# Gates projected with channels on the partitions, probabilities divided by their sums on GpSimd, masks in bias rows, a new beginning and a finer selection in a two-layer streaming encoder step

## What is computed

```python
h = rmsnorm(x, g_norm[l]);  p = split_proj(h @ w_in[l])
# A: every query keeps its top-k keys by an indexer's score, and attends to them
score = einsum('bqh,bqhl->bql', wi, relu(dots));  top_s, top_i = lax.top_k(score, topk)
# B: logits + F[t] - F[s], F = cumsum(log_sigmoid(..)), causal
# C: own chunk of 64 and eight before it, a learned bias on t - s
# M: cross-attention into 256 memory tokens
prob = softmax(where(mask, q @ k.T * HEAD_DIM ** -0.5 + bias, -inf));  o = prob @ v
x = x + concat([o_a * silu(p['a_g']), o_b * silu(p['b_g']), o_c * silu(p['c_g']), o_m * silu(p['m_g'])]) @ w_out[l]
```

## Time and profile before

| | us |
|---|---|
| median of three runs (lowest, highest) | 1735.61 (1731.92, 1735.61) |
| the profiled execution | 1734.48 |
| its span, first to last instruction | 1732.6 |
| busy: TensorE / VectorE / ScalarE / GpSimd | 1701.1 / 1009.0 / 665.2 / 225.8 |

### The profile page before, as it was taken

One profiled execution on the slowest core, in us unless ns is written; L12 is line 12 of the kernel. 1 busy time (PEld: TensorE's weight loads), 2 busy tenths in 40 slices (PEclk: granted clock), 3 DMA queues, 4 the chain that ended last, 5 costly groups with the idle time before them and its releaser, 6 DMA issues.

```text
span 1732.6 us, 30341 instructions
## 1 busy us (share of the span) xinstructions
PE 1701.1 (98%) x10922; PEld 1113.2 (64%) x10922; DVE 1009.0 (58%) x2709; ACT 665.2 (38%) x1599; POOL 225.8 (13%) x424
## 2 busy tenths in 40 slices
PE   6999999999999999999999999999999999999998
PEld 3566777767778755555444677767777786555553
DVE  3645878878788333332235378887888872333322
ACT  3542334323343345454124323343333433445531
POOL 1233321100010000001012422210000000000000
PEclk9999999999999999999999999999999999999999
DMA  7434322323132323113421533241231324221020
GB/s 253 121 136 127 126 92 75 110 77 104 41 125 92 102 71 100 37 44 91 121 100 50 166 101 125 93 137 41 80 107 38 122 95 119 63 88 48 33 85 37
DMA packets 53716, 163.36 MB, mean 94 GB/s; under 512 B 9456, under 2 KB 23632, under 8 KB 51008
## 3 DMA queue, kind: packets, MB, share of 16 engines
q1 hardware_dynamic: 39424, 125.88, 22.3%
q0 software_dynamic: 14144, 35.54, 6.1%
HBM read 134.41 MB, written 30.07 MB: 95 GB/s over the span
## 4 chain that ended last, share of the span: by engine, by line
PE 89%; DVE 7%; DMA 2%; issue 1%; ACT 1%; DVEq 0%; ACTq 0%; SPq 0%
PE psX L844 60%; PE psT L791 8%; PE psS L960 6%; PE psX L1027 6%; DVE lower L1242 2%; PE psS L872 2%; DMA wring<-in_w 1%; PE psX L1002 1%; PE psS L791 1%; DVE sc L1405 1%; PE psX L791 1%; PE psS L933 1%; PE psS L926 0%; DMA scratch_xres<-xr 0%; DVE work L1463 0%
## 5 line engine op out<-in xcount | busy, mean ns | idle before, releaser
L844 PE MATMUL psX<-wring,hT 128*128 128x512 f32 (+2 forms) x2016 | 835.1, 558 | 5.8 <-DMA wring<-in_w 2.7
L844 PEld LDWEIGHTS psX<-wring,hT 128*128 128x128 f32 x2016 | 364.7, 190 | 326.4 <-issue 315.5
L1242 DVE TENSOR_SCALAR_CACHE_REDUCE lower<-sc,thr 128x640 uint8<-128x640 f32 (+5 forms) x462 | 407.3, 934 | 16.9 <-issue 9.3
L844 PE MATMUL psX<-hT,wring 128*128 128x128 f32 x2880 | 336.0, 276 | 4.8 <-ACT gate L1139 4.8
L844 PEld LDWEIGHTS psX<-hT,wring 128*128 128x128 f32 x2880 | 329.2, 193 | 7.2 <-issue 6.6
L1181 ACT ACTIVATE work<-work,stat 128x256 f32<-128x256 f32 (+7 forms) x288 | 200.0, 695 | 289.1 <-DVEq L1466 286.7
L1190 ACT COPY work<-psT 128x512 f32<-128x512 f32 (+2 forms) x352 | 156.9, 488 | 332.7 <-PE psT L791 331.9
L791 PEld LDWEIGHTS psT<-con,work 128*128 128x128 f32 x1080 | 122.2, 141 | 70.1 <-issue 65.3
L791 PE MATMUL psT<-con,work 128*128 128x128 f32 x1080 | 157.3, 278 | 0.0
L1463 DVE CUSTOM_DVE_ANT_0 work<-psS,bias 128x640 f32<-128x640 f32 (+7 forms) x112 | 79.6, 711 | 34.1 <-issue 19.0
L1463 DVE CUSTOM_DVE_ANT_0 work<-psS,sc 128x384 f32<-128x384 f32 (+5 forms) x48 | 42.8, 891 | 72.6 <-PE psT L791 70.8
(11 more groups left out here) (203 smaller groups left out, 1550.6 us busy)
## 6 DMA issues: line engine op xcount, KB each, us to landing
wring<-in_w SPq DMA_DIRECT2D x20, 2048.0 KB, 9.3
cache<-in_kB SPq DMA_DIRECT2D x16, 512.0 KB, 6.1
cache<-in_vB SPq DMA_DIRECT2D x16, 512.0 KB, 4.3
cache<-in_kC SPq DMA_DIRECT2D x16, 512.0 KB, 6.3
cache<-in_vC SPq DMA_DIRECT2D x16, 512.0 KB, 4.5
scratch_oscr<-gate POOLq DMA_DIRECT2D x54, 128.0 KB, 2.0
hT<-scratch_oscr SPq DMA_DIRECT2D x18, 384.0 KB, 3.6
kv<-in_x SPq DMA_DIRECT2D x9, 512.0 KB, 5.7
```

The costliest lines, as they stand in the source:

```text
L844: mm = pe.matmul(out, lhs, rhs, start=(kt == 0), stop=(kt == KT - 1))
L1242: v.tensor_scalar(lower[:, at:at + STRIP_L[t]], sc[:, o], thr[:, n:n + 1], 0.0, ALU.is_lt, ALU.add, accum_out=below[:, n:n + 1])
```

## The change

- Gates first in B2, C2 and A2, and turned, as is the whole of M1: the gates come out with channels on the partitions. V and GT transpose none of them; R computes in this layout.
- Z moves into the pack's own unit, behind the second half of its selection. VectorE inverts the sums of even and odd heads one after the other, GpSimd multiplies the probabilities of prompt packs by them in place, and T waits for that (`weighed`). Request packs keep their scaling in V on VectorE.
- The masks of requests: GpSimd adds them to the bias rows (`close_samples`); for A the selection of `ST_` is stored to memory and loaded as bias rows.
- Beginning: the identity is loaded apart, the first 3 x 512 columns of A1 apart (behind tile 0), ScalarE runs a Sqrt and TensorE four matmuls over zeros meanwhile; `turn 0` before `norm 1`. B1 comes in two halves.
- The step `ranks` is split in `equals` and `ranks`, with new costs.

```diff
-TURNED = {"mm": 2, "B1": 4, "C1": 4, "M1": 2}
+TURNED = {"mm": 2, "B1": 4, "B2": 2, "C1": 4, "C2": 2, "M1": 4, "A2": 2}
...
 out = [(kind, i) for i in range(32) for kind in ("bit", "rest")]
-return out + [("bit", 32)] + [(kind, t) for t in [ST_] + SEL_TILES for kind in ("ranks", "mask")]
...
 count = lambda part: sum(STRIP_L[t] / 960 + 0.25 for t in part)
 cost = lambda x: {"bit": 0.5 + count(FIRST) * (x[1] < 32), "rest": count(REST)}.get(
-    x[0], (3.3 if x[0] == "ranks" else 2.2) * STRIP_L.get(x[1], 0) / 960 + 0.5)
+    x[0], {"equals": 1.9, "ranks": 2.2, "mask": 2.4}.get(x[0], 0) * STRIP_L.get(x[1], 0) / 960 + 0.5)
...
-if prev:
-    emit("Z", prev)
...
+def weigh():
+    if pipe[0] and not weighed[0]:
+        emit("Z", pipe[0])
+        weighed[0] = True
 def settle():
     odd_heads()
+    weigh()
+    weighed[0] = False
     old = pipe.pop()
...
+weigh()
 emit("P", c, t)
...
-emit("con")
+emit("ident")
 emit("gn")
+emit("head")
 emit("X", ("x", 1))
 emit("W", "A1")
+emit("con")
 emit("X", ("x", 2))
 emit("X", ("x", 3))
 emit("gm")
 emit("W", "mm")
 emit("norm", 0)
+emit("turn", 0)
 emit("norm", 1)
-emit("turn", 0)
 late = []
...
-    sp.dma_start(wring[:, i % 2, :], rows(d["w"], l, len(CHUNKS) * P, CHUNKS.index(s[1]) * P, P)
-                 ).then_inc(w_loaded[i % 2].sem, 16)
+    src = rows(d["w"], l, len(CHUNKS) * P, CHUNKS.index(s[1]) * P, P)
+    begin = 0 if i else 3 * 512
+    if s[1] == "B1":
+        place = wring[:, i % 2, :].rearrange("p (k c) -> p k c", k=KT)
+        src = src.rearrange("p (k c) -> p k c", k=KT)
+        sp.dma_start(place[:, :, 0:W], src[:, :, 0:W]).then_inc(half_loaded.sem, 16)
+        sp.dma_start(place[:, :, W:2 * W], src[:, :, W:2 * W]).then_inc(w_loaded[i % 2].sem, 16)
+        continue
+    sp.dma_start(wring[:, i % 2, begin:], src[:, begin:]).then_inc(w_loaded[i % 2].sem, 16)
 elif k == "CL":
     u = s[1]
     i = cache_loads.index((l, u))
...
+for _ in range(4):
+    pe.matmul(psX[:, 0, :], om[:, 0, :], om[:, :, :].rearrange("p j c -> p (j c)"), start=True, stop=True)
+pe.wait_ge(s_ident, 16)
...
         mm = pe.matmul(o[64 * r:64 * r + 64, 0:n], qs[:, j % 2, 64 * r:64 * r + 64],
-                       kc[0][:, r * n:(r + 1) * n], start=True, stop=False)
-    pe.wait_ge(*selj_ready.on(s[1]))
-    sm = sc[:, SC_OFF[ST_]:SC_OFF[ST_] + SKEYS]
-    pe.wait_ge(*selected.on(ST_))
-    pe.matmul(o[:, 0:n], selj[:, :], sm[:, 0:n], start=False, stop=True)
-    pe.matmul(o[:, n:SKEYS], qs[:, j % 2, :], kA[:, 1, SEQ:TOK], start=True, stop=False)
-    mm = pe.matmul(o[:, n:SKEYS], selj[:, :], sm[:, n:SKEYS], start=False, stop=True)
+                       kc[0][:, r * n:(r + 1) * n], start=True, stop=True)
+    mm = pe.matmul(o[:, n:SKEYS], qs[:, j % 2, :], kA[:, 1, SEQ:TOK], start=True, stop=True)
 else:
...
-        mm = pe.matmul(o[:, n:SKEYS], ident, con[:, base + 96 - 32 * j:base + 96 - 32 * j + P],
-                       start=False, stop=True)
+            mm = pe.matmul(o[part, n:SKEYS], qs[:, j % 2, part], kT[:, g, SEQ:TOK], start=True, stop=True)
 mm.then_inc(S.fill(u).sem, 1)
...
 p, hp = s[1:]
-pe.wait_ge(*probs.on((p, [i for i in range(heads(p)) if i % 2 == hp][-1])))
+if is_sample(p):
+    pe.wait_ge(*probs.on((p, 0)))
+else:
+    pe.wait_ge(*weighed.on((p, hp)))
...
 pe.wait_ge(*pt_act.on(p))
-pe.wait_ge(*scaled.on(p))
 if br in "BC":
...
-for i in range(0, nh, 2):
-    g = (h0 + i) // 2
-    turn(o[:, W + i // 2 * P:W + (i // 2 + 1) * P], gates(br)[:, t, g * P:(g + 1) * P])
...
+mm = pe.matmul(X.ap(s)[:, g * P + 32 * j:g * P + 32 * j + 32], om[:, j, :],
+               con[:, C_SELG + 32 * g:C_SELG + 32 * g + 32], start=True, stop=True)
...
+xg, rest = (x[:, W:2 * W], None) if c == "M1" else (x[:, 0:W], x[:, W:2 * W])
 if c in ("B2", "C2"):
-    nc.scalar.copy(vX[:, t, :], x[:, 0:W])
+    nc.scalar.copy(vX[:, t, :], rest)
 elif c == "A2":
-    nc.scalar.copy(sg[:, 0:W], x[:, 0:W])
...
-br, t, h0, nh = s[1]
-act.wait_ge(*X.fill(s).on(s))
-nc.scalar.copy(merged(br, t, h0 // 2, nh // 2),
-               X.ap(s)[:, W:W + nh * HD].rearrange("p (g c) -> p g c", g=nh // 2))
-act.drain().then_inc(g_turned.sem, 1)
...
+if s[1][0] == "equals":
     count_below([t])
     v.tensor_scalar(eq, a, thr[:, n:n + 1], -BIG, ALU.is_equal, ALU.mult)
     dve.drain()
+    continue
+if s[1][0] == "ranks":
     v.tensor_tensor_scan(a, eq, eq, 0.0, ALU.add, ALU.bypass)
...
-    if br == "B" or h0 == 0:
-        dve.wait_ge(*sbias.on((br, h0)))
-    if br == "C" and h0 == 0:
-        v.tensor_copy(sbias_[:, PAST + STEPS:SKEYS].rearrange("p (b i) -> p b i", i=STEPS),
-                      sbias_[:, PAST:PAST + STEPS].unsqueeze(1).to_broadcast([P, 7, STEPS]))
-        dve.drain()
+    dve.wait_ge(*closed.on((br, h0)))
+    b_ = sbias_[:, 0:L]
+elif is_sample(p) and br == "A":
...
 n = heads(p)
-dve.wait_ge(*probs.on((p, n - 1)))
-v.reciprocal(stats(p)[:, 2, 0:n], stats(p)[:, 1, 0:n])
+for hp in buffers(p):
+    dve.wait_ge(*probs.on((p, [i for i in range(n) if i % 2 == hp][-1])))
+    last = v.reciprocal(stats(p)[:, 2, hp:n:2], stats(p)[:, 1, hp:n:2])
+    if not is_sample(p):
+        last.then_inc(inverted.sem, 1)
 dve.drain()
-if not is_sample(p):
-    ga = gates(br)[:, t, h0 * HD:(h0 + n) * HD].rearrange("p (h d) -> p h d", h=n)
-    v.tensor_tensor(ga, ga, stats(p)[:, 2, 0:n].unsqueeze(2).to_broadcast([P, n, HD]), ALU.mult)
-    dve.drain()
-dve.drain().then_inc(scaled.sem, 1)
...
-dve.wait_ge(*g_turned.on(s[1]))
-o = merged(br, t, h0 // 2, nh // 2)
-v.tensor_tensor(o, X.ap(s)[:, 0:nh * HD].rearrange("p (g c) -> p g c", g=nh // 2), o, ALU.mult
+ga = gates(br)[:, t, h0 * HD:(h0 + nh) * HD].rearrange("p (g c) -> p g c", g=nh // 2)
+v.tensor_tensor(merged(br, t, h0 // 2, nh // 2),
...
 elif k == "R":
     dve.wait_ge(*X.fill(s).on(s))
-    ga = gates(s[1])[:, ST_, :]
-    v.tensor_tensor(ga, X.ap(s)[:, 0:W], ga, ALU.mult).then_inc(X.empty(s).sem, 1)
+    two = lambda ap: ap.rearrange("p (g c) -> p g c", g=2)
+    v.tensor_tensor(merged(s[1], ST_, 0, 2), two(X.ap(s)[:, 0:W]), two(gates(s[1])[:, ST_, :]), ALU.mult
+                    ).then_inc(X.empty(s).sem, 1)
     dve.drain().then_inc(gated.sem, 1)
...
+    src = bass.AP(d["sm"].tensor, (2 * j + r) * STEPS * SKEYS, [[0, H], [SKEYS, STEPS], [1, SKEYS]])
 else:
...
+    cols = sbias_[:, PAST:SKEYS]
+    if br == "B":
+        pool.wait_ge(*sbias.on((br, j)))
+        g.tensor_tensor(cols, cols, con[:, C_CAUS + 96 - 32 * j:C_CAUS + 96 - 32 * j + P], ALU.add
+                        ).then_inc(closed.sem, 1)
+        return
+    if j == 0:
+        pool.wait_ge(*sbias.on((br, 0)))
+        g.tensor_copy(own[:, :], cols[:, 0:STEPS])
+        pool.drain()
+    by_request = lambda ap: ap.rearrange("p (b i) -> p b i", i=STEPS)
+    g.tensor_tensor(by_request(cols), own[:, :].unsqueeze(1).to_broadcast([P, R, STEPS]),
+                    by_request(con[:, C_FULL + 96 - 32 * j:C_FULL + 96 - 32 * j + P]), ALU.add
+                    ).then_inc(closed.sem, 1)
 for l, s in order:
...
-if br == "A":
-    g.tensor_scalar(selj[:, :], con[:, C_SELT:C_SELT + P], con[:, C_PM + j:C_PM + j + 1], None,
-                    ALU.mult).then_inc(selj_ready.sem, 1)
-elif br == "B" and j == 0:
+if br == "B" and j == 0:
...
+    if br == "B" and j == 0:
+        close_samples("B", 0)
+    elif br == "A" and j == 0:
+        pool.wait_ge(*logits.on((last_sample["C"], 0)))
+        pool.wait_ge(*sm_stored.on("s"))
+        sample_bias("A", 0)
+elif k == "K" and s[1] == ("mask", ST_):
+    pool.wait_ge(*selected.on(ST_))
+    store(d["sm"], sc[:, SC_OFF[ST_]:SC_OFF[ST_] + SKEYS], sm_stored.sem)
+elif k == "T" and is_sample(s[1]) and s[1][0] == "B":
+    close_samples(*[("B", s[1][2] + 1), ("C", 0)][s[1][2] == PAIRS - 1])
 elif k == "L" and s[2] == buffers(s[1])[-1]:
     p = s[1]
...
     sample_bias(*sbias_loads[h0 + 1])
+elif br in "CA" and is_sample(p) and h0 < PAIRS - 1:
+    pool.wait_ge(*logits.on(last_logits))
+    if br == "C":
+        close_samples("C", h0 + 1)
+    else:
+        sample_bias("A", h0 + 1)
...
+elif k == "Z" and not is_sample(s[1]):
+    p = s[1]
+    for hp in buffers(p):
+        pool.wait_ge(*inverted.on((p, hp)))
+        for i in range(hp, heads(p), 2):
+            x = buf(hp)[:, offset(p, i):offset(p, i) + blocks(p) * P]
+            last = g.tensor_scalar(x, x, stats(p)[:, 2, i:i + 1], None, ALU.mult)
+        last.then_inc(weighed.sem, 1)
```

More of the change, by code:

```diff
@@ L124, in topk_steps @@
     out = [(kind, i) for i in range(32) for kind in ("bit", "rest")]
-    return out + [("bit", 32)] + [(kind, t) for t in [ST_] + SEL_TILES for kind in ("ranks", "mask")]
+    return out + [("bit", 32)] + [(kind, t) for t in [ST_] + SEL_TILES for kind in ("equals", "ranks", "mask")]
 def program_order():
@@ L136, in program_order @@
     to_turn = []
-    gather = []
     odd = []
     pace = [0.0]
+    weighed = [False]
     def emit(*s, ahead=0):
@@ L207, in settle @@
             emit("R", old[0])
-            gather.append(old[0])
     def project(c, t):
```

(35 more changed lines are left out.)

79 lines of the change are left out of this document (42 added, 37 removed).

## The result

| kernel | time, us | runs | profiled execution: time / span, us | mean granted clock |
|---|---|---|---|---|
| before | 1734.90 median (1731.92 to 1735.61) | 4 | 1734.48 / 1732.6 | 0.998 |
| changed | 1895.72 median (1893.90 to 1897.14) | 4 | 1897.14 / 1895.0 | 0.968 |

A forecast was written before the change was run, and what follows sets the result against it. The prediction took TensorE to be the bound everywhere, with no slack. From 1734.5 us it took off 21.2 for the small terms and added 138.6 of waits and 15 of clock: 1866.9, called 1866, range 1770 to 1915.

The forecast's parts named there:

- forecast case: In the selection's units TensorE's T waits for GpSimd's division behind the counts: 1866 us (1815 to 1915), chance 0.63.
- rival 1: At T, the same wait but a cheap GpSimd, 640 columns near the copy's 0.75 us: 1781 to 1798 us, chance 0.22.
- rival 2: Z isn't late, GpSimd's multiplication runs under P, V and S, only the -21 us are left: 1713 us, chance 0.08.
- the sign: At the kernel's beginning, the projection A1 of tile 0 would be over near 19 us.
- gates turned: Projection in B2, C2, A2 and M1: narrower matmuls cost +0.13 us for each of 54 and 18 units, +9.4 together.
- gate transposes of V: In every V, 128 gate transposes of about 0.11 us go: -14.1 us.
- R: In R, 16 full-width weight loads at 0.11 us replace narrow ones, eight times: +9.5 us, bounds 0 to +9.5.
- finer selection: In M1, splitting ranks in two clears two stalls of about 2.4 us and a slow stretch: -6.3 us, other end 0.
- waits at T: TensorE's T in the selection's units waits for GpSimd's division: 138.6 us in both layers, bounds 68 and 165.
- lower clock: On TensorE behind long waits: half of about twenty waits cost 1.5 us each, +15 us, bounds 0 and 40.
- lateness plus 0.45 plus GpSimd: Each pack's wait at T: counts' end minus T's old start, 0.45 us for reciprocal and handovers, GpSimd's even-head time.
- the recovery: In four-head packs of B and C, waiting TensorE takes back VectorE's lag: 0.6 us lateness remains, 26.1 us; without it 39.

The follow-up runs named there:

- e_best: Changed kernel with even heads' reciprocals ahead of odd heads and behind only the first selection step, B's bias rows behind the odd heads' multiplication: 1725.9 us.
- e_nodiv: Changed kernel without the division: GpSimd multiplies nothing and T waits for the exponentials again, all else of the change stays; 1717.2 us.
- e_coarse: On top of e_nodiv, the selection's count and scan in one step again, at the old cost; 1720.7 us.
- e_half: Changed kernel with GpSimd multiplying only the first half of each head's columns, all waits kept; 1831.8 us.
- e_split: Changed kernel with Z in two: even heads' reciprocals ahead of the unit's second selection step, odd heads' behind it; 1784.3 us.
- e_order: Against e_split, the even half of Z moved ahead of T and L of the odd heads; 1735.5 us.

## Why the prediction was right, and where it was off

**The mechanism.** Z is late, in the selection's units, behind the counts; the packs pay anew each time; behind the selection nothing waits. All of that stands in the trace as forecast (behind the selection one T waits, 0.28 us). The forecast case, not a rival, is what happened; rival 1 fell with the row of 1929 ns, rival 2 would have needed Z in another place (e_best is nearly that kernel, 1725.9 instead of 1713). One reading was wrong: 22.44 in the earlier trace rows stands in the projection of tile 1. TensorE leaves that of tile 0 at 21.40 in the kernel before and at 16.98 in the changed one, where the sign said near 19; the gain, 4.4 us, lies in the bounds.

**The sum, term by term.** The small terms are measured from start to start on TensorE, in e_nodiv against the kernel before; the beginning is the time of the first transposes of a projected tile, 28.40 before, 22.77 in e_nodiv, 23.98 in the changed kernel. Waits move between neighbours, so the rows need not add up to the line below them exactly. The same beginning came at 22.77, 23.98 and 25.41 us in three executions, so its row is good to a few us only.

| term | forecast, us | measured, us |
|---|---|---|
| gates turned (54 and 18 units) | +9.4 | +16.3 for the whole projection |
| gate transposes of V | -14.1 | -22.2 |
| GT | -1.8 | -1.7 |
| R | +9.5 | +9.3 |
| masks of B and C | -4.3 | -5.2 |
| masks of A | -8.6 | -8.7 |
| beginning | -5 | -5.6 (-4.4 in the changed kernel) |
| finer selection | -6.3 | -3.5 by e_coarse |
| new waits of S for VectorE's turned tiles | 0 | +3.4 |
| the rest together | -21.2 | -18.2 (spans), -18.7 (medians) |
| waits at T | +138.6 | +138.3 by the sum above, +133.5 against e_nodiv |
| lower clock | +15 (0 to 40) | +47 |

- *Gates.* The 256-column halves take 0.22 us from start to start (514.26 to 515.13 for four), not half of 0.43; with 3.60 and 3.58 against 6.88 a unit costs 0.30 more, not 0.13. The other way round, a gate transpose took 0.173 in the kernel before (22.2 us for 128), not 0.11, and V did not get slower when they went: what I had left with V as the switch to 64 columns of the array was theirs. The two errors nearly cancel (-5.9 against -4.7).
- *R.* 16 loads of full width for 32 columns. Loads and streams by form, R of e_nodiv: 128 times 14.7 / 128 = 0.115 us from start to start, where the forecast had 0.11. The bound of zero, a narrow stream that isn't held to its weights, is out. The changed kernel's row of these loads:

```profile
L1061 PEld LDWEIGHTS psX<-con,om 128*128 128x128 f32 x128 | 15.1, 192 | 2.7 <-issue 2.7
```

  The Trainium skill ("TensorE: Matmul & The Clock Gate", "LDWEIGHTS (loading the stationary operand)") says that a load's time goes by its columns, not its rows. The trace agrees that it grows with the columns, 192 ns for 128 here against 109 ns for the 32 of the kernel before, but not in proportion to them; no run here changes the rows.
- *Waits at T.* The mechanism for each pack, lateness plus 0.45 plus GpSimd, measured 2.28 from the end of the count to T in the unit shown, against 2.39. What was mis-sized: four-head packs, where I took only 0.6 us of lateness to remain (26 us a layer, measured 33; without the recovery the prediction had 39), and B's wide packs, forecast 21, measured 16.
- *Clock.* This is the term that was mis-sized, by 32 us, and with it all of the miss of 30 us (the rest together gained 3 less than forecast, the waits against e_nodiv came out 5 less). I counted about twenty waits of 2.5 us and more and let half of them cost 1.5 us; 23 of the 26 waits above 2.4 us had a stretch at the lower level, and it cost some 2 us each (47 us over 23 stretches). I had two waits of 2.4 us to go by the earlier trace rows, one with and one without, and used them for waits twice as long. Its upper bound, 40, was too low too; the range held because other bounds were wide.

**What the prediction underrated.** It took the division's place and its price as one thing. e_half, e_split and e_order part them: half of the price gives 64 us back, another place in the same queues 160.

Left open: why S now waits three times for VectorE's turned tiles (3.4 us in all); no kernel here tries it. Of the 8.7 us between e_best and e_nodiv, 7.0 are waits at T; the rest is within what the medians scatter.

## What to carry to other kernels

When a step is handed to a slow but idle engine, ask first behind what its input is computed, and what is queued ahead of it on the engine that takes it: here 380 us of GpSimd's work cost 178 us in one place of two in-order queues and about 9 in another. On a kernel bound by TensorE, price a wait of several microseconds at its own length and about 2 us more for the clock, if it is as long as those here (3.4 us and more, where all 18 had a slow stretch), and look for such waits before shaving instructions. An engine whose queue also holds urgent copies (ScalarE's out of psX) was a bad place for a step that waits, in both orders tried, though it did the step faster (0.82 against 1.93 us for 640 columns).

## What the runs showed of the hardware that I had not expected

- The lower clock came at every wait of TensorE of 3.4 us and more (18 of 18) and most above 2.4 us (5 of 8), and transposes of a constant put into the waits cut the stretches at the lower level from 122.7 to 47.7 us in all.
- GpSimd's multiplication by a scalar of each partition is linear from 128 to 1024 f32 columns: 0.27 us and 2.54 ns a column, 1566 ns for 512, where its copy took 600 for 511. ScalarE's takes 819 ns for 640 columns.
- A transpose between the projection and matmuls with 64 columns of weights took 0.173 us from start to start, against 0.11 to 0.12 in a row of transposes: 8 us over the 128 that went.
